# Attention scores of two heads per half tile, alternating between row halves of the matmul array, in a two-layer hybrid attention and PEER kernel

## What is computed

```python
proj = jnp.einsum('bld,dk->blk', x, w_in)          # aq ak av bq bk bv cq ck cv dq dk dv iq ik iw
# group A: 8 heads, sliding window of 128, two key heads, with sinks
# group B: 4 heads, softmax(q1 k1) - lam * softmax(q2 k2), values of width 128
# group C: 8 heads, three dilations in one mixture
# group D: 8 heads, one key head; the indexer picks the 64 keys of each query
sc = relu(einsum('bhqd,bsd->bqhs', iq, ik) * IDX_DIM ** -0.5)    # 8 indexer heads
score = einsum('bqh,bqhs->bqs', iw * IDX_HEADS ** -0.5, sc)
_, idx = lax.top_k(score, topk)
mixed = concatenate([A, B, C, D]);  y = mixed @ w_out
x = layer_norm(ALPHA * x + y);  x = layer_norm(ALPHA * x + peer_ffn(x))
```

## Time and profile before

| | us |
|---|---|
| three timed runs, median | 3992.87 |
| lowest, highest | 3989.93, 3992.98 |
| the profiled execution, its own time | 3993.01 |
| its span, first to last instruction | 3991.2 |
| matmul busy, all lines | 3932.5 |
| VectorE, ScalarE, GpSimd busy | 2644.5, 1987.7, 507.7 |
| mean granted clock of TensorE | 0.995 |

### The profile page before, as it was taken

One profiled execution on the slowest core, in us unless ns is written; L12 is line 12 of the kernel. 1 busy time (PEld: TensorE's weight loads), 2 busy tenths in 40 slices (PEclk: granted clock), 3 DMA queues, 4 the chain that ended last, 5 costly groups with the idle time before them and its releaser, 6 DMA issues. The chain is left out here.

```text
span 3991.2 us, 63940 instructions
## 1 busy us (share of the span) xinstructions
PE 3932.5 (99%) x20356; PEld 3326.4 (83%) x20356; DVE 2644.5 (66%) x5020; ACT 1987.7 (50%) x2846; POOL 507.7 (13%) x716
## 2 busy tenths in 40 slices
PE   8999999999999999999999999999999999999997
PEld 7778888888888888888777788888888888888886
DVE  6655678658865555555676556886588655555556
ACT  4554544654565444444455545456545654444443
POOL 1000000640072000000010000007301720000000
PEclk9999999999999999999999999999999999999999
DMA  6435556559645666666554354564596456666665
GB/s 221 144 120 203 177 187 208 173 188 292 215 169 189 241 232 229 226 232 228 212 173 142 124 204 175 194 204 175 194 282 212 176 203 229 230 230 225 231 230 207
DMA packets 244353, 810.89 MB, mean 203 GB/s; under 512 B 24976, under 2 KB 157584, under 8 KB 158864
## 3 DMA queue, kind: packets, MB, share of 16 engines
q1 hardware_dynamic: 207376, 775.84, 56.0%
q10 hardware_dynamic: 36864, 33.57, 2.4%
HBM read 756.89 MB, written 52.43 MB: 203 GB/s over the span
## 5 line engine op out<-in xcount | busy, mean ns | idle before, releaser
L1047 DVE TENSOR_TENSOR lo<-raw,hi 128x1024 fp32r<-128x1024 f32 x1312 | 1617.9, 1233 | 1010.3 <-ACT hi L724 979.5
L724 ACT ACTIVATE hi<-raw 128x1024 fp32r<-128x1024 f32 x1312 | 1388.5, 1059 | 1509.6 <-PE bank L678 756.8
L460 PE MATMUL bank<-xhl,hi 128*128 128x512 f32 x4608 | 1631.4, 398 | 1.8 <-ACT scr L879 1.4
L461 PE MATMUL bank<-xhl,lo 128*128 128x256 f32 x4608 | 1290.1, 280 | 0.0
L460 PEld LDWEIGHTS bank<-xhl,hi 128*128 128x128 f32 x4608 | 866.1, 188 | 202.0 <-ACT scr L879 1.8
L461 PEld LDWEIGHTS bank<-xhl,lo 128*128 128x128 f32 x4608 | 870.8, 189 | 0.0
L676 PE MATMUL bank<-hi,xhl 128*128 128x512 f32 x2048 | 797.9, 390 | 3.0 <-DVE gelu_out L1341 2.6
L678 PE MATMUL bank<-hi,xhl 128*128 128x512 f32 x2048 | 797.5, 389 | 0.0
L677 PE MATMUL bank<-lo,xhl 128*128 128x512 f32 x2048 | 797.5, 389 | 0.0
L676 PEld LDWEIGHTS bank<-hi,xhl 128*128 128x128 f32 x2048 | 384.5, 188 | 83.9 <-DVE gelu_out L1341 3.3
L678 PEld LDWEIGHTS bank<-hi,xhl 128*128 128x128 f32 x2048 | 384.5, 188 | 79.7
(11 more groups left out here) (143 smaller groups left out, 2438.3 us busy)
## 6 DMA issues: line engine op xcount, KB each, us to landing
raw<-u_t SPq DMA_DIRECT2D x256, 1024.0 KB, 5.0
raw<-v_t SPq DMA_DIRECT2D x256, 1024.0 KB, 4.8
raw<-w_in SPq DMA_DIRECT2D x84, 1024.0 KB, 4.8
raw<-w_out SPq DMA_DIRECT2D x32, 1024.0 KB, 4.7
raw<-wq SPq DMA_DIRECT2D x32, 1024.0 KB, 4.8
gelu_scratch<-gelu_out ACTq DMA_DIRECT2D x256, 128.0 KB, 3.9
scr<-gelu_scratch SPq DMA_DIRECT2D x256, 128.0 KB, 4.6
gates_scratch<-arena SPq DMA_DIRECT2D x32, 512.0 KB, 9.9
```

What stands on the lines that cost most here:

```text
L460: pe.matmul(acc[:], wh, xhl[:, c, :, :].rearrange("p a t -> p (a t)"), start=(c == 0), stop=False)
L461: return pe.matmul(acc[:, L:2 * L], wl, xh[:, c, :], start=False, stop=(c == DC - 1))
L724: act.activation(hi[j % NSPLIT][:], half, ACT.Copy).then_inc(hi_done, 1)
L1047: dve.tensor_tensor(lo[j % NSPLIT][:], half, hi[j % NSPLIT][:].bitcast(F32), ALU.subtract).then_inc(lo_done, 1)
```

## The change

The score items come in pairs, two heads of the same group (or the two parts of one head of B) in one slot: 20 slots instead of 40, with new numbers in `SCORE_AT`, and `TOP_AT` one earlier. Within a pair the source's four matmuls go block by block, head by head, so that they alternate between rows 0 to 63 and rows 64 to 127. The first head of a pair writes bank 4, the second bank 5. The pair waits until both items of the pair before it were read, and counts the semaphore `scored` up by two at its last matmul. The readers do both items of a pair in the slot, one after the other; the transposes keep their rule, one burst per slot.

```diff
-SCORE_AT = {"I": (21, 22, 23, 24, 25, 26, 27, 28), "A": (29, 31, 34, 36, 38, 39, 44, 46),
-            "D": (50, 51, 52, 55, 58, 59, 62, 65), "B": (53, 54, 56, 57, 60, 61, 63, 64),
-            "C": (69, 70, 71, 72, 73, 74, 75, 76)}
+SCORE_AT = {"I": (21, 23, 25, 27), "A": (28, 31, 36, 39), "D": (48, 52, 55, 60), "B": (54, 57, 62, 64), "C": (69, 71, 73, 75)}
-TOP_AT = 30
+TOP_AT = 29
...
-    for t, n in sorted(at.items()):
-        kind, h, part = items[n]
-        if kind == "I" or (kind == "B" and part == 0):
-            continue
-        free = t + 2
-        while free in slots:
-            free += 1
-        slots[free] = (kind, h, 0)
+    for t, pair in sorted(at.items()):
+        for n in pair:
+            kind, h, part = items[n]
+            if kind == "I" or (kind == "B" and part == 0):
+                continue
+            free = t + 2
+            while free in slots:
+                free += 1
+            slots[free] = (kind, h, 0)
...
-                    def scores(n):
-
-                        kind, h, part = ITEMS[n]
-                        qp, kp, half = score_operands(kind, h, part)
-                        rows = slice(HD * half, HD * half + HD)
+                    def scores(pair):
+
+                        kind = ITEMS[pair[0]][0]
                         pe.wait_ge(staged_read, TURN_NO["rope", ROPED_FOR[kind], NB - 1] + 1)
-                        if n >= 2 and n - 2 < N_INDEX:
-                            pe.wait_ge(irelu, n - 1)
-                        elif n >= 2:
-                            pe.wait_ge(masked_done, NB * (head_item(n) - 1))
+                        if 0 < pair[0] <= N_INDEX:
+                            pe.wait_ge(irelu, pair[0])
+                        elif pair[0]:
+                            pe.wait_ge(masked_done, NB * head_item(pair[0]))
                         for b in range(NB):
-                            last = pe.matmul(bank[4 + n % 2][:, block_cols[b]], qk_t[rows, qp, b * P:(b + 1) * P],
-                                             qk_t[rows, kp, 0:(b + 1) * P], start=True, stop=True)
-                        last.then_inc(scored, 1)
+                            for n in pair:
+                                qp, kp, half = score_operands(*ITEMS[n])
+                                rows = slice(HD * half, HD * half + HD)
+                                last = pe.matmul(bank[4 + n % 2][:, block_cols[b]], qk_t[rows, qp, b * P:(b + 1) * P],
+                                                 qk_t[rows, kp, 0:(b + 1) * P], start=True, stop=True)
+                        last.then_inc(scored, 2)
...
-                        if t in ITEM_AT and ITEM_AT[t] >= N_INDEX:
-                            row_max(ITEM_AT[t])
+                        for n in ITEM_AT.get(t, ()):
+                            if n >= N_INDEX:
+                                row_max(n)
```

More of the change, by code:

```diff
@@ L75, in score_items @@
     items = []
[L76 to L79, removed]
+    for t, kind, i in sorted((t, kind, i) for kind, slots in SCORE_AT.items() for i, t in enumerate(slots)):
+        items += [(t, kind, i, part) if kind == "B" else (t, kind, 2 * i + part, 0) for part in range(2)]
+    return [item[1:] for item in items], {item[0]: (n - 1, n) for n, item in enumerate(items) if n % 2}
 def rope_turn_at(r, b):
@@ L131, in build @@
     ITEMS, ITEM_AT = score_items()
-    N_INDEX = len(SCORE_AT["I"])
+    N_INDEX = 2 * len(SCORE_AT["I"])
     N_HEAD_ITEMS = len(ITEMS) - N_INDEX
@@ L840, in _ @@
                         if t in ITEM_AT:
[L841 to L844, removed]
+                            for n in ITEM_AT[t]:
+                                if n < N_INDEX:
+                                    relu(n)
+                                else:
+                                    exps(n)
                     for m in range(HPG + AHEAD, N_OUT):
@@ L1257, in _ @@
                     for t in range(AHEAD, N_SLOTS):
-                        if t - 1 in ITEM_AT and ITEM_AT[t - 1] >= N_INDEX:
-                            row_sums(ITEM_AT[t - 1])
+                        for n in ITEM_AT.get(t - 1, ()):
+                            if n >= N_INDEX:
+                                row_sums(n)
                         if t >= HPG and (t - HPG) % HPG < NB and (t - HPG) // HPG < N_ROPED:
                             rotate((t - HPG) // HPG, (t - HPG) % HPG)
-                        if t in ITEM_AT and ITEM_AT[t] >= N_INDEX:
-                            row_max(ITEM_AT[t])
+                        for n in ITEM_AT.get(t, ()):
+                            if n >= N_INDEX:
+                                row_max(n)
                         if t in VALUE_AT:
                             take_out(*VALUE_AT[t])
-                        if t - 1 in ITEM_AT and ITEM_AT[t - 1] < N_INDEX:
-                            indexer_add(ITEM_AT[t - 1])
+                        for n in ITEM_AT.get(t - 1, ()):
+                            if n < N_INDEX:
+                                indexer_add(n)
                         if 0 <= t - TOP_AT < TOP_STEPS:
```

## The result

The changed kernel takes 3950.8 us (median of four runs, 3947.7 to 3952.7) against 3992.6 us before (median of four as well): a ratio of 0.9896, with an interval from 0.9879 to 0.9913. That is 41.8 us less.

What follows compares the result with a forecast made beforehand. TensorE's own queue was taken as the bound. Per layer 20 x (2 x 1.08 - P) - 1.1, over two layers 84.2 - 40P, with P = 1.51 saved 23.8 us: 3969 us, range 3958 to 3979 us.

Steps and rivals of the forecast that it cites:

- What bounds the kernel: In the stage with the scores: TensorE's own queue, busy 264.00 us of 264.00; what it sheds shortens the run one for one.
- The fixed cost of 0.43 us per item: Gaps and bare loads around each score burst: paid 20 times a layer instead of 40; a pair 1.73 us against 2.16.
- The alternation: Inside a pair's burst: records of the two row halves overlap partly, with loads still 0.11 us apart; a pair costs 1.51 us.
- P: TensorE time that one pair of score items costs; taken as 1.51 us, bounded between 1.08 and 2.32 us.
- rival 1: Score bursts: the two halves run together, loads as well; P = 1.29, saving 32.6 us, 3960 us; chance 0.27.
- 84.2 - 40P: Saving in us over two layers, from 20 x (2 x 1.08 - P) - 1.1 per layer.
- columns halve entirely, 1.08 us a pair: Lower end for a pair's burst: full halving, 3952 us; given a little of rival 1's chance of 0.27.
- Skipped company: Transposition bursts that now stand alone, no longer behind a score item, cost more: 1.1 us a layer lost.
- The waits: Pairs waiting for both banks to be read, tightest at pairs 54 to 55 and 27 to 28: put at nothing.
- Rival 2: Score bursts: no overlap at all, only half as many bursts; P = 1.73, saving 15.0 us, 3978 us; chance 0.18.
- rivals 3 and 4: Within pairs: row-half changes drain the engine, 4002 us, 0.07; or nearly nothing saved, by 0.09 us drains or bank waits, 0.07.
- Rival 3: Between the four twos of records of every pair: drains of 3 x 0.20 us, P = 2.32, 8.6 us longer; chance 0.07.

Runs made afterwards that it cites:

- same_rows: Changed kernel with both heads of a pair taken from rows 0 to 63, so without the second row half; 3976.8 us, ratio 0.9967.
- full_rows: Changed kernel with the scores contracted over all 128 rows, so without a change of row count; 3962.0 us, ratio 0.9929.
- heads_in_turn: Changed kernel with head A's two blocks first, then head B's; 3950.0 us, ratio 0.9897.
- crossed_blocks: Changed kernel with the order head A block 1, head B block 0, head A block 0, head B block 1; 3952.2 us, ratio 0.9904.
- twice_in_turn: Changed kernel with every score matmul done twice, all of head A's before head B's; 4007.1 us, ratio 1.0040.

## Why the prediction was wrong, point by point

**What bounds the kernel, and that a shorter queue of TensorE shortens the run one for one: right.** Two stages of 20.1 us less make 40.2 of the 41 us.

**The fixed cost of 0.43 us per item, paid half as often: right.** same_rows measured 1.73 us for a pair as worked out, and full_rows showed what it is: 0.37 us of it is the change of row count.

**The alternation: wrong, and this is the step that failed.** The prediction took P = 1.51 us, "since it keeps the only pace of loads that the scores show". That pace, one load per 0.11 us, is the pace of one row half; no row before had two halves in it, and the pace was carried over to both together. Measured is P = 1.09: the loads of the two halves run side by side. The second half of the step failed as well, in the forecast and in rival 1 alike: "Matmuls start in program order", taken record by record, so that head B could begin only beside head A's second record and its last 0.216 us step was left over behind head A's. Here head B's first record starts about 0.01 us after head A's, and in heads_in_turn still does so past two matmuls of head A. Of rival 1, the statement on loads held, and its 1.29 us did not: it is 0.20 us too long, that left-over step. With P = 1.09 the prediction's own formula, 84.2 - 40P, gives 40.6 us, against 41.8 measured between the medians and 41.0 between the profiled executions. The end of the bounds that proved true was named, "columns halve entirely, 1.08 us a pair", and given a little of rival 1's 0.27; its 3952 us was left out of the range. The price was bounded rightly and weighed wrongly: the lower end had a reason of its own (two halves that share no rows), the value taken had only the habit of one half.

The Trainium skill, TensorEngine Tiling (Array Packing), section Key Properties, said just that: different tiles load weights and multiply in parallel. The trace of the changed kernel agrees to the hundredth (four records 0.92 us, eight 0.93). The 1.29 us that rival 1 put beside the rule gave it less overlap than it states.

**Skipped company: right in kind, short in size.** Bursts that stand alone now do cost their own entry. Over a stage, 243.91 us less 68 half tiles of 2.72 us less 20 x 1.09 us leaves 37.2 us for transposes and values; before it was 263.99 - 184.96 - 43.2 = 35.8. That is 1.4 us a layer for 1.1 forecast; the values, whose half tiles also lost their scores, were left out of the forecast, and whether they are the whole rest was not measured.

**The waits: right, nothing waits.** The tight place on VectorE, the last masked minimum of pair 54 and what follows it, and the bursts of pairs 54 and 55:

```profile
192.21 0.42 DVE L1193 CUSTOM_DVE_ANT_0 scr<-bank,arena 128x256 f32<-128x256 f32 x1
...
192.55 0.29 DVE L1244 TENSOR_TENSOR arena<-bank,st 128x128 f32<-128x128 f32 x1
```

```profile
190.35 0.93 PE L498 MATMUL bank<-arena 64*128 64x128 f32 x8
...
195.12 0.93 PE L498 MATMUL bank<-arena 64*128 64x128 f32 x8
```

The last bank is read by 192.6 us, the next pair starts at 195.12: 2.5 us clear, for 1.3 at least forecast. And on ScalarE, the two rectified copies of pair 27 and the burst of pair 28:

```profile
99.51 0.87 ACT L790 ACTIVATE scr<-bank 128x384 f32<-128x384 f32 x2
```

```profile
101.67 0.93 PE L498 MATMUL bank<-arena 64*128 64x128 f32 x8
```

Through at 99.51 + 0.87 = 100.38 us, 1.3 us before 101.67, for 1.1 forecast. Evacuation did not become the bound, not even with four items.

**Rivals 2, 3 and 4: all refuted.** Rival 2 is what same_rows measured, the burst without overlap: 1.73 us for 1.09. Against rivals 3 and 4, a change of row half inside a burst costs nothing that the trace can show. (Rival 3's three changes of 0.20 us make 0.60 and P = 2.33 us, not 2.32; nothing hangs on it.)

## What to carry to other kernels

Fp32 matmuls that contract over 64 rows should be issued in pairs on rows 0 to 63 and 64 to 127, into different banks as here: the second took no time of its own (eight records in 0.93 us for four in 0.92). With two matmuls per half the order hardly matters; with four of one half in a row, the other half stood still for 0.76 us (a burst of 2.50 us for 1.73), so long bursts should alternate. Gather them in as few bursts as the banks allow, since each trip from 128 rows to 64 and back cost 0.37 us. When a price has no row in the trace, ask which resource the nearest row measures, one half or both, before its pace is carried over.

## What the runs showed of the hardware that was not expected

- The two row halves start within about 0.01 us of each other, weight loads too, and each keeps its own pace.
- Order across the halves is not kept. In crossed_blocks a matmul written second was, by the profile's modelled ends, through while the first still ran, and the one written fourth had started before the third. A semaphore counted up by the last matmul of a burst therefore says of itself nothing on the other half; here the two halves have the same work and end together. No run here let a reader come too early, so that is a caution, not a finding. The Trainium skill, TensorE: Matmul & The Clock Gate, section Part 3: Packing small matmuls, says that matmuls start and end in program order, so that one count on the last is sound. For two row halves the starts of crossed_blocks (head B's 256-wide matmul before head A's 128-wide one) and of heads_in_turn (head B's first 0.01 us behind head A's first and before its second) show otherwise, and the measurement decides; that the last matmul written ended before another, no run shows.
- The rule that fits the runs: each half takes one running and one waiting source matmul (of two records each), and what finds no place holds up the other half too. Two in a row held up nothing (heads_in_turn); four held up the other half's first for 0.76 us (77.36 to 78.12 in twice_in_turn). Three were not run.
- The change from 128 rows to 64 and back cost 0.37 us of 1.73; scores on all rows entered the projection stream without a gap.
